# Two transformer blocks on one core: convolution taps, layer norm, biases and a gated sum of the second block in another order

## The reference

```python
for l in range(DEPTH):                                    # DEPTH = 2
    h = modulate(rmsnorm(x, norm1_g[l]), sh1, sc1)        # hc likewise for the context
    a, naq, nak, nav, gq, gk, gv, gates = split_in(h @ w_in[l])
    # branch a: gated linear unit, convolution of 31 taps, layer norm, silu
    u = a[..., :512] * sigmoid(a[..., 512:])
    y = depthwise_conv31(u, conv_w[l]) + conv_b[l]
    br_a = silu(layernorm(y, conv_ln_g[l], conv_ln_b[l])) @ w_conv_out[l]
    # branch b: 8 heads, neighbourhood attention with a bias table and a mask
    br_b = na_latent(naq, nak, nav, context keys and values, na_rpb[l]) @ w_na_out[l]
    # branch c: 8 query heads on 2 key heads, rms norm and rotation of q and k
    br_c = gqa_latent(q, k, gv, context keys and values) @ w_gqa_out[l]
    y2 = sigmoid(ga) * br_a + sigmoid(gb) * br_b + sigmoid(gc) * br_c
    x = x + g1 * (y2 @ w_out[l])
    x = x + g2 * swiglu(modulate(rmsnorm(x, norm2_g[l]), sh2, sc2), w_ffn_in[l], w_ffn_out[l])
    # in layer 0 the context goes through the same branches, with dense attention
```

## Time and profile before

| | us |
|---|---|
| median of 3 runs | 3115.95 |
| lowest, highest | 3101.68, 3116.22 |
| profiled execution | 3107.96 |
| its span in the trace | 3106.2 |
| PE busy | 2886.0 |
| DVE busy | 1724.0 |
| ACT busy | 1142.0 |
| POOL busy | 381.9 |

### The profile page before, as it was taken

One profiled execution on the slowest core, in us unless ns is written; L12 is line 12 of the kernel. 1 busy time (PEld: TensorE's weight loads), 2 busy tenths in 40 slices (PEclk: granted clock), 3 DMA queues, 4 the chain that ended last, 5 costly groups with the idle time before them and its releaser, 6 DMA issues.

```text
span 3106.2 us, 38090 instructions
## 1 busy us (share of the span) xinstructions
PE 2886.0 (93%) x16134; PEld 2403.3 (77%) x16134; DVE 1724.0 (56%) x2381; ACT 1142.0 (37%) x1515; POOL 381.9 (12%) x331
## 2 busy tenths in 40 slices
PE   6999988999999998899979979998999989899998
PEld 5888666888888876678869856657887868878887
DVE  6842223387685213238766964334756748854674
ACT  4421202344443121134432344443434433465442
POOL 2300010032230001003300420110000000422000
PEclk8999978999999998899999989999999999999999
DMA  6554645355555355535523321223554533334552
GB/s 198 187 176 127 203 136 163 122 177 180 181 180 191 113 190 163 163 109 176 197 74 95 98 62 58 67 69 123 190 179 160 183 116 109 110 110 121 190 187 99
DMA packets 442031, 445.10 MB, mean 143 GB/s; under 512 B 13679, under 2 KB 433640, under 8 KB 441862
## 3 DMA queue, kind: packets, MB, share of 16 engines
q1 hardware_dynamic: 436320, 434.86, 43.2%
q0 software_dynamic: 2400, 5.40, 0.7%
q10 hardware_dynamic: 3142, 2.41, 0.3%
HBM read 441.46 MB, written 1.17 MB: 143 GB/s over the span
## 4 chain that ended last, share of the span: by engine, by line
PE 84%; DVE 9%; ACT 4%; issue 1%; POOL 1%; DMA 1%; ACTq 0%; SPq 0%; DVEq 0%
PE bank L1496 27%; PE bank L1497 14%; PE bank L1545 12%; PE bank L1458 11%; PE bank L1555 8%; PE bank L1491 3%; DVE R L2415 2%; PE bank L1662 2%; PE bank L1865 1%; DVE lower L679 1%; PE bank L1669 1%; PE bank L1603 1%; PE bank L1856 1%; PE bank L1739 1%; DVE lower L1985 1%
## 5 line engine op out<-in xcount | busy, mean ns | idle before, releaser
L1496 PE MATMUL bank<-h_pair,upper 128*128 128x512 f32 x2464 | 874.9, 400 | 37.5 <-DVE h_pair L2016 18.7
L1985 DVE TENSOR_TENSOR lower<-ring,upper 128x2048 fp32r<-128x2048 f32 (+1 forms) x238 | 569.7, 2396 | 292.9 <-ACT upper L1009 292.9
L1497 PE MATMUL bank<-h_pair,lower 128*128 128x256 f32 x2464 | 692.8, 281 | 0.0
L1009 ACT ACTIVATE upper<-ring 128x2048 fp32r<-128x2048 f32 (+1 forms) x238 | 441.4, 1863 | 495.7 <-PE bank L1497 495.7
L1496 PEld LDWEIGHTS bank<-h_pair,upper 128*128 128x128 f32 x2464 | 466.7, 189 | 153.0 <-issue 35.2
L1497 PEld LDWEIGHTS bank<-h_pair,lower 128*128 128x128 f32 x2464 | 468.9, 190 | 0.2
L1496 PE MATMUL bank<-hid_pair,upper 128*128 128x512 f32 x1232 | 432.1, 396 | 0.0
L1497 PE MATMUL bank<-hid_pair,lower 128*128 128x256 f32 x1232 | 344.5, 280 | 0.0
L1496 PEld LDWEIGHTS bank<-hid_pair,upper 128*128 128x128 f32 x1232 | 231.2, 188 | 55.5
L1555 PE MATMUL bank<-ring,hT 128*128 128x256 f32 (+2 forms) x1024 | 241.4, 400 | 30.2 <-ACT Q L1078 19.7
L1545 PE MATMUL bank<-hT,ring 128*128 128x256 f32 x1152 | 255.6, 384 | 12.4 <-DVE hT L1975 11.4
(11 more groups left out here) (283 smaller groups left out, 3860.1 us busy)
## 6 DMA issues: line engine op xcount, KB each, us to landing
ring<-in_w_ffn_in SPq DMA_DIRECT2D x154, 1024.0 KB, 5.0
ring<-in_w_ffn_out SPq DMA_DIRECT2D x56, 1024.0 KB, 5.1
ring<-in_w_mix_in SPq DMA_DIRECT2D x48, 1024.0 KB, 5.2
ring<-in_w_mod SPq DMA_DIRECT2D x48, 1024.0 KB, 5.3
ring<-in_w_in SPq DMA_DIRECT2D x42, 1024.0 KB, 5.2
ring<-in_w_ffn_out SPq DMA_DIRECT2D x28, 768.0 KB, 4.5
ring<-in_w_mix_out SPq DMA_DIRECT2D x16, 1024.0 KB, 5.2
ring<-in_w_in SPq DMA_DIRECT2D x16, 512.0 KB, 5.1
```

The lines of the kernel that those rows point to most:

```text
L1009: act.activation(f.upper(p)[:, 0:n], slot[:, 0:n], ACT.Copy).then_inc(up_ready, 1)
L1496: pe.matmul(bank[:, 0:2 * T], up[:, cols], x_pair.rearrange("p e t -> p (e t)"), start=first, stop=False)
L1497: return pe.matmul(bank[:, 0:T], low[:, cols], x_pair[:, 0, :], start=False, stop=last)
L1985: dve.tensor_tensor(f.lower(p)[:, 0:n], slot[:, 0:n], f.upper(p)[:, 0:n].bitcast(F32), ALU.subtract)\
```

## The change

Five things are changed, in block 2 alone. The work and its results' formulas are the same.

- *Taps.* `tap(c, k)` issues tap k of one chunk, and waits for tap k - 1 of that chunk alone (`taps_at`). `next_tap` takes, among the chunks whose glu item has been gated and that still have taps, the one whose last tap was issued longest ago. The table `LEAD` gives for each layer and each glu item how many taps are issued there and what stands between them. All 124 are issued ahead of the attention: 33 ahead of the fourth glu item in layer 0, 25 in layer 1.
- *Layer norm.* `weave` puts `mean` at step 1 and `var` at step 4 in layer 0 (6 and 9 before), and at -1 and 2 in layer 1 (3 and 6 before). In layer 0 branch a's outputs begin at step 9 (11 before).
- *Biases.* Heads 0 and 1 are loaded ahead of the rotation, then heads n and n + 1 together, after both adds of the pair before.
- *Lower parts of y2.* They are made item by item: parts 0 and 1 after gated item 1, 2 and 3 after item 2, 4 and 5 after item 3, then 6 and 7, then the lower part of piece 32. ACT makes the upper half of piece 32 after part 3 of `y2_up`.
- ACT's loop begins at step -1, for the `mean` of layer 1.

```diff
+LEAD = [[[8, (LOW, 3), 2], [10, (LOW, 4), 2], [9, (LOW, 5), 2],
+         [10, (LOW, 6), 12, (LOW, 7), 13, (LOW, 8), 7, (SUMS, 0), (SUMS, 1), 4, (LOW, 9), 6, (SUMS, 2), (SUMS, 3), 5,
+          (LOW, 10), 7, (NORMS, 0), (LOW, 11), 8, (LOW, 12), 7, (LOW, 13), 9, (LOW, 14), 3]],
+        [[11], [2, (LOW, 3), 5], [2, (LOW, 4), 5],
+         [2, (LOW, 5), 9, (LOW, 6), 24, (LOW, 7), 9, (LOW, 8), 1, (SUMS, 0), (SUMS, 1), 5, (LOW, 9), 10, (SUMS, 2),
+          (SUMS, 3), 10, (LOW, 10), 11, (NORMS, 0), 5, (LOW, 11), 13, (LOW, 12), (LOW, 13), (LOW, 14)]]]
...
     at = -1
-    for n in range(3):
-        if last and n == 2:
-            at = put(at, "mean", 0, 0, 1)
+    if last:
+        at = put(at, "mean", 0, 0, 1)
+    at = put(at, "gate", 0, 0, 2)
+    at = put(at, "var" if last else "mean", 0, 0, 1)
+    at = put(at, "gate", 0, 1, 2)
+    if not last:
+        at = put(at, "var", 0, 0, 1)
+    for n in (2, 3):
         at = put(at, "gate", 0, n, 2)
-    at = put(at if last else at + 1, "var" if last else "mean", 0, 0, 1)
-    at = put(at, "gate", 0, 3, 2)
-    if not last:
-        at = put(at, "var", 0, 0, 1) + 1
     for n in range(4):
         at = put(at, "branch", 0, n, 1 if last else 2)
     for n in range(4):
-        at = put(at, "gate", 1, n, 2)
+        at = put(at, "gate", 1, n, 4 if not last and n == 3 else 2)
...
                     if s == 0:
                         load_bias(0)
+                        load_bias(1)
...
                 for n in range(NA_UNITS):
-                    if n + 1 < NA_UNITS:
+                    if n % 2 == 0 and n:
+                        load_bias(n)
                         load_bias(n + 1)
                     pool.wait_ge(bias_landed[n % 2], 32 * (bias_n // 2 + 1))
...
                 up_of(31)
-                up_of(32)
                 for m in range(KD):
                     act.wait_ge(y2_ready, 16 * layer + 8 + m + 1)
                     act.activation(y2_up[:, m, 0:nT], y2[:, m, 0:nT], ACT.Copy).then_inc(y2_up_ready, 1)
+                    if m == 3:
+                        up_of(32)
...
+                def tap(c, k):
 
                     if k:
-                        chain.settle()
-                    for c in range(KC2):
...
+                        dve.wait_ge(dve_done, chain.base + taps_at[c, k - 1])
...
+                def next_tap(ready, n_issued):
+
+                    c = min((c for c in range(ready) if taps[c] < TAPS2), key=lambda c: issued[c])
+                    if taps[c] == 0:
+                        evicted(dve, item + c)
+                    tap(c, taps[c])
+                    taps[c] += 1
+                    issued[c] = n_issued
...
                 for n in range(4):
                     gated_branch(2, n)
-                    if n % 2:
-                        low_of(31 + n // 2)
-                for m in range(KD):
+                    if n == 1:
+                        low_of(31)
+                    if n:
+                        y2_low_part(2 * n - 2)
+                        y2_low_part(2 * n - 1)
+                y2_low_part(6)
+                y2_low_part(7)
+                low_of(32)
```

More of the change, by code:

```diff
@@ L188 @@
 DVE_START, DVE_CHAIN1, POOL_CHAIN1 = 18, 91, 20
[L191 to L199, removed]
+LOW, SUMS, NORMS = "low", "sums", "norms"
+LEAD = [[[8, (LOW, 3), 2], [10, (LOW, 4), 2], [9, (LOW, 5), 2],
[4 more added lines that the diff above has]
+          (SUMS, 3), 10, (LOW, 10), 11, (NORMS, 0), 5, (LOW, 11), 13, (LOW, 12), (LOW, 13), (LOW, 14)]]]
+assert all(sum(n for steps in layer for n in steps if isinstance(n, int)) == KC2 * TAPS2 for layer in LEAD)
 def weave(layer):
@@ L1361, in norm_part @@
                     act.activation(lroot[:, 0:nT], src, func, bias=bias, scale=1.0 / CONV2).then_inc(pair_free[it % 2], 1)
-                for i in range(max(WEAVES[layer]) + 1):
+                for i in range(-1, max(WEAVES[layer]) + 1):
                     j = i // 2
@@ new lines, in _ @@
+                taps, taps_at, issued = [0] * KC2, {}, [-1] * KC2
+                def tap(c, k):
+                    if k:
+                        dve.wait_ge(dve_done, chain.base + taps_at[c, k - 1])
+                    src = bass.AP(R, 4096 + c * cin_pitch + k, [[12288, P], [HALO + T, nh], [1, T]])
+                    dst = cout[:, c, 0:nT].rearrange("p (h t) -> p h t", h=nh)
+                    w = pcol("conv_w_2", (layer * TAPS2 + k) * KC2 + c)
+                    if k == 0:
+                        ins = dve.tensor_scalar(dst, src, w, pcol("conv_b_2", KC2 * layer + c), ALU.mult, ALU.add)
+                    else:
+                        ins = dve.scalar_tensor_tensor(out=dst, in0=src, scalar=w, in1=dst, op0=ALU.mult, op1=ALU.add)
+                    if k == TAPS2 - 1:
+                        ins.then_inc(cout_ready, 1)
+                    else:
+                        chain(ins)
+                        taps_at[c, k] = chain.n
@@ L2441, in g_norms @@
                            .then_inc(g_normed, 1)
-                for k in range(LEAD_TAPS[layer]):
-                    for what, n in LEAD_STEPS[layer].get(k, ()):
-                        if what == "low":
-                            low_of(n)
-                        elif what == "gss":
-                            g_sums(n)
+                n_issued = 0
+                for n in range(4):
+                    glu_gated(item + n, n, nT, glu0, cin_dst(n))
+                    for step in LEAD[layer][n]:
+                        if isinstance(step, int):
+                            for _ in range(step):
+                                next_tap(n + 1, n_issued)
+                                n_issued += 1
+                        elif step[0] == LOW:
+                            low_of(step[1])
+                        elif step[0] == SUMS:
+                            g_sums(step[1])
                         else:
                             g_norms()
-                    tap(k)
-                taps_done = LEAD_TAPS[layer]
+                glu0 += 4
                 def gated_branch(b, n):
@@ L2491, in _ @@
                                .then_inc(lnorm_ready, 1)
-                    if i < len(TAPS_AT_UNITS[layer]):
-                        for _ in range(TAPS_AT_UNITS[layer][i]):
-                            tap(taps_done)
-                            taps_done += 1
                     if here:
@@ L2506, in _ @@
                                       ALU.subtract).then_inc(y2_split, 1)
+                for n in range(4):
+                    gated_branch(2, n)
+                    if n == 1:
[6 more added lines that the diff above has]
+                low_of(32)
                 for n in range(4):
```

22 lines of the change are left out of this document (1 added, 21 removed).

## The result

The changed kernel takes 3056.09 us (median of 4 runs, 3051.87 to 3066.4) where the kernel before, measured with it, takes 3113.24 (4 runs, 3101.68 to 3116.22). The medians lie 57 us apart. The ratio, estimated from the runs of both kernels, is 0.9845, with a 95% interval of 0.9823 to 0.9866, which is 48 us less (55 to 42). The profiled execution has a span of 3055.4 us where it was 3106.2, 50.8 less. So the gain is about 50 us, and a total time tells it no closer than to some 7 us. The forecast was 3063, with 3046 to 3090 around it, and 47.9 us of gain in its sum.

A forecast was written before the change was run, and what follows sets the result against it. TensorE, busy 93%, bounds the kernel; only its waits and slow clock in block 2 can be won. 25.0 + 7.8 - 1.5 + 10.4 + 6.2 = 47.9 us gives 3060.1 or 3068.0; forecast 3063, range 3046 to 3090.

The forecast's parts named there:

- Layer 0's attention, 25.0 us: Layer 0's attention: PE's three waits, 19.0 us, and slow clock of 4.05 and 1.9 go; bounds 17 and 27.
- The end of the gated sum, 7.8 and 6.2 us: Gated sum's end: waits for y2's lower parts go, 7.8 us in layer 0 (4 to 8), 6.2 in layer 1 (3 to 7).
- Layer 1 ahead of the attention, -1.5 us: Layer 1 before attention: 3.6 us wait and 1.7 go, piece 12 costs 4.9 and 1.9; bounds +4 and -4.
- Layer 1's attention, 10.4 us: Layer 1's attention: of 11.0 us idle and 4.7 slow, 3.8 and 1.5 remain; gain 10.4, bounds 4 and 15.7.
- The price of a tap: VectorE's convolution taps: 0.1 us per dependence met at once; layer 1's 13 taps take 8.8 us without GpSimd.
- (a): Rival: layer 1's waits only change place and part of layer 0's stays; gain 24 to 34 us, 3074 to 3092; chance 0.19.
- (b): Rival: the bias chain of masks, loads and adds becomes the bound, slower, about 3140 us; chance 0.04.
- (c): Rival: early taps push the glu stage's lower parts, PE waits there, half to all gain lost, 3080 to 3115; chance 0.07.
- (d): Rival: better than forecast, layer 1's loop loses its waits too and piece 12 comes in time, 3040 to 3052; chance 0.10.

The follow-up runs named there:

- the fourth experiment: The kernel before with only the biases by pairs and y2's lower parts item by item, taps, layer norm and step table as before: 3066.44 us, ratio 0.9881.
- the spread-out kernel: The changed kernel with layer 1's last 18 taps placed none, 8, 5, 5 around the lower parts instead of 5, 13, 0, 0: 3047.53 us, once more 3051.13.
- The sixth experiment: The changed kernel with taps always of the lowest chunk that has any left, so nearly each waits for the one directly ahead: 3062.96 us, ratio 0.9857.
- the seventh experiment: The changed kernel with the mask added to each bias three times instead of once on GpSimd: 3065.16 us, ratio 0.9865.

## Why the prediction was right, and where it was not

*Layer 0's attention, 25.0 us.* Measured: 30.9 us for the stage, of which 5.9 are y2's, so 25.0. All three waits of the earlier trace rows went, no new one came, and the clock is 1.00. The experiments divide it: the step table 12.3 us (the Silu's wait and its slow stretch, forecast 10.6 + 1.9 = 12.5), the remaining 12.7 us to taps and biases together. The sum was right, and one reading in it was not: the prediction laid the 6.8 us wait to 6.30 us of taps and one bias of 1.66. In the trace three waits for a bias lie ahead of it, and the biases alone took 4.8 us out of it (the fourth experiment). Since all taps and all late biases were to go, this did no harm here. The two overlap: with the taps in their old place the biases are worth 6.1 us, with the taps gone nothing.

*The end of the gated sum, 7.8 and 6.2 us.* Measured 7.5 and 6.5 by taking it back. Two rows, a wait and half of the busy time at the lower clock, were enough.

*Layer 1 ahead of the attention, -1.5 us.* Measured -0.9 in this pair of executions. Over all executions named above the two orders lie 1 to 7 us apart, so that the bound of -4 is not ruled out, and the near hit is partly luck. The step was wrong: the prediction let the 3.6 us wait for piece 11 go, since VectorE was 21 taps ahead, and charged 4.9 us for piece 12. In fact piece 11's lower part came 2.67 us late and piece 12's 2.05. The five taps between the norms of G and piece 11 took 4.93 us in the shared stretch, and I had set that part's end to the moment at which PE begins to wait instead of adding up to it. The mechanism, taps queued ahead of a lower part where each costs 1 us, is what the spread-out kernel shows.

*Layer 1's attention, 10.4 us.* Measured 18.3 - 5.5 = 12.7. The size was near, the cause wrong. The prediction gave the first wait to taps and bias and half of the others to the loop of VectorE and ScalarE, and valued the biases by pairs at nothing beside the other terms, or a loss of up to 1.5 us. Taken back from the changed kernel they are worth 11.3 us, and put into the kernel before 8.2; the old step table is worth 0.8, taps and norm together 4.6 with the biases changed. The step that failed is the one that read "DVE waits 1.66 us for its bias" as something that other terms contain. In layer 1 six such waits, 10 us of VectorE, sit in a loop that is as long as PE's period, and they came out as 11.3 us of PE.

*The price of a tap.* The prediction took 0.1 us for a dependence from 6.30/8 = 0.79 us a tap against 0.69, and 0.68 us for a tap of 256 columns without GpSimd from four in 2.72 us. Neither row shows that. These are the two groups, ns min/median/max:

```profile
L2415 DVE SCALAR_TENSOR_TENSOR R<-R,params x8: 739/747/1545, 1781.4 to 1786.9; 128x512 f32<-128x512 f32 x8
...
L2415 DVE SCALAR_TENSOR_TENSOR R<-R,params x4: 472/473/1540, 2691.1 to 2693.3; 128x256 f32<-128x256 f32 x4
```

In each group one tap runs beside GpSimd's add of the mask and takes 0.8 to 1.1 us longer; that one tap is most of the excess. The sixth experiment gives 0.12 us for the dependence, so the 0.1 was right by luck. A tap of 256 columns alone costs 0.40 us, ten in 4.04, so the 13 taps would have taken some 5 us without GpSimd and not 8.8.

*The rivals.* (a), that layer 1's waits only change place, did happen ahead of the attention and nowhere else. (b), the bias chain as the bound, did not: landings were 3.0 us in the median in layer 1 and 2.7 in layer 0, and DVE waited once, for 0.5 us. The third addition of the mask agrees with where the limit was said to be, close in layer 1 and far in layer 0. (c) did not come: the glu stage has 4.8 us of idle time of DVE left of 28.5 and no wait of PE. (d) came by half: the attention of layer 1 gave more than forecast, though less than its good bound of 15.7, the stage ahead of it only in the spread-out kernel, which at 3047.53 us lies in the range given for (d).

*Chance in it.* The sum of 47.9 us lies 0.3 from the ratio's 48.2, 2.9 from the 50.8 between the spans, 4.4 from the 52.3 of the stages and 9 from the medians' 57. The first of these is no better a test than the others, and the agreement to 0.3 us is luck. What bears the prediction out are the stages: 25.0 for 25.0, 7.5 and 6.5 for 7.8 and 6.2, with the waits that were named, and 12.7 for 10.4 and -0.9 for -1.5 with other causes.

## What to carry to other kernels

Value a wait of a helper engine by the loop that it sits in: where that loop is shorter than the bound engine's period it is worth nothing, and where it is as long it may all arrive. The same 1.66 us was both in one kernel; how much arrives in between (a third in the seventh experiment) has to be measured. Behind one wait of PE several rounds of the loop can stand, so follow it back over more than one. Two causes ahead of one wait don't add up when undone one by one, so undo each alone and from the other side as well. When work is moved into an idle stretch, check what it is queued ahead of, item by item, with the duration that it has in that stretch and not elsewhere. And compare two stretches only after counting that they hold the same work.

## What the runs showed of the hardware

A VectorE instruction that waits for the one directly ahead started 0.12 us later than one that needs an older result (0.79 against 0.66 us from tap to tap, 128x512). Beside work of GpSimd VectorE's instructions took longer. A tap of 128x256 took 12.91/13 = 0.99 us in a row of them, where it takes 0.40 alone (ten in 4.04 us), and a lower part 2.96 instead of 2.28. Beside a single add of the mask, 0.75 us on GpSimd, one tap took 1.54 where its neighbours took 0.47. This decided which of two orders of the same taps was free in layer 1. And code that was the same took up to 7 us more or less from one execution to another (405.6 to 412.7 us in the FFN part), as much as some of the effects of a single edit here, with no cause shown.
